# Low parts of the expert tables in the gate stage: from VectorE to GpSimd

## The reference

```python
act = jax.nn.gelu(jnp.einsum('td,tkd->tk', hx, u_tab[ix]))
return jnp.einsum('tk,tkd->td', gx * act, v_tab[ix])
```

## Time and profile before

| what | value |
|---|---|
| median of 3 runs | 3313.42 us (3311.34 to 3317.97) |
| the profiled execution, own time | 3313.91 us |
| its span | 3312.1 us, mean granted TensorE clock 0.951 |
| busy: TensorE / VectorE / ScalarE / GpSimd | 2998.8 / 2008.9 / 1268.6 / 138.2 us |
| gate stage, layer 0 and layer 1 | 531 to 677 us, 2221 to 2366 us |

### The profile page before, as it was taken

One profiled execution on the slowest core, in us unless ns is written; L12 is line 12 of the kernel. 1 busy time (PEld: TensorE's weight loads), 2 busy tenths in 40 slices (PEclk: granted clock), 3 DMA queues, 4 the chain that ended last, 5 costly groups with the idle time before them and its releaser, 6 DMA issues. The chain is left out here.

```text
span 3312.1 us, 48668 instructions
## 1 busy us (share of the span) xinstructions
PE 2998.8 (91%) x17552; PEld 2692.5 (81%) x17552; DVE 2008.9 (61%) x3884; ACT 1268.6 (38%) x1854; POOL 138.2 (4%) x108
## 2 busy tenths in 40 slices
PE   7957897899999999999877767987899999999997
PEld 4946797799999999988666666987899999999885
DVE  8867589944446666655569843789744444444454
ACT  3342445743333333333421124447633333333333
POOL 0000350000000000000000001510000000000000
PEclk9977899999999999999888877999999999999999
DMA  5703233664466666656300021325754444444463
GB/s 201 267 19 118 89 115 121 254 218 151 150 202 214 214 214 214 214 152 177 114 14 10 3 94 54 109 96 217 263 160 150 151 151 150 150 150 151 138 178 110
DMA packets 308862, 489.98 MB, mean 148 GB/s; under 512 B 214256, under 2 KB 215024, under 8 KB 304256
## 3 DMA queue, kind: packets, MB, share of 16 engines
q1 hardware_dynamic: 305856, 438.02, 40.8%
q10 hardware_dynamic: 2880, 50.33, 3.8%
HBM read 430.91 MB, written 57.38 MB: 147 GB/s over the span
## 5 line engine op out<-in xcount | busy, mean ns | idle before, releaser
L163 DVE TENSOR_TENSOR val_vl<-val_vr,val_vh 128x1024 fp32r<-128x1024 f32 x256 | 313.8, 1226 | 882.7 <-ACT val_vh L1828 882.7
L1665 PE MATMUL pe_s<-peer_hi,pe_uh 128*128 128x384 f32 x2304 | 784.8, 341 | 26.8 <-DVE peer_lo L163 15.9
L1667 PE MATMUL pe_s<-peer_hi,pe_ul 128*128 128x384 f32 x2304 | 775.9, 337 | 0.0
L1666 PE MATMUL pe_s<-peer_lo,pe_uh 128*128 128x384 f32 x2304 | 775.8, 337 | 0.0
L1763 ACT ACTIVATE pe_A<-pe_s 128x384 f32 (+1 forms) x256 | 126.1, 493 | 1124.2 <-PE pe_s L1667 1124.2
L1730 PE MATMUL peer_acc<-val_vh,val_wl 128*128 128x512 f32 x1536 | 474.2, 390 | 0.0
L1665 PEld LDWEIGHTS pe_s<-peer_hi,pe_uh 128*128 128x128 f32 x2304 | 436.5, 189 | 45.7 <-issue 23.0
L1730 PE MATMUL peer_acc<-val_vh,val_wh 128*128 128x512 f32 x1536 | 473.2, 389 | 0.0
L1730 PE MATMUL peer_acc<-val_vl,val_wh 128*128 128x512 f32 x1536 | 472.7, 389 | 0.0
L1666 PEld LDWEIGHTS pe_s<-peer_lo,pe_uh 128*128 128x128 f32 x2304 | 436.9, 190 | 8.4
L1667 PEld LDWEIGHTS pe_s<-peer_hi,pe_ul 128*128 128x128 f32 x2304 | 436.4, 189 | 0.0
(11 more groups left out here) (436 smaller groups left out, 3528.1 us busy)
## 6 DMA issues: line engine op xcount, KB each, us to landing
pe_ur<-in_peer_u SPq DMA_DIRECT2D x256, 512.0 KB, 3.6
val_vr<-in_peer_v SPq DMA_DIRECT2D x256, 512.0 KB, 4.4
val_gr<-gates SPq DMA_DIRECT2D x256, 192.0 KB, 4.6
val_mrow<-in_ada_rows SPq DMA_DIRECT2D x56, 512.0 KB, 4.1
gates<-gate_stg ACTq DMA_DIRECT2D x6, 4096.0 KB, 13.5
pe_ur<-in_w_query SPq DMA_DIRECT2D x32, 512.0 KB, 3.5
gates<-gate_stg ACTq DMA_DIRECT2D x4, 3072.0 KB, 12.8
in_w<-in_w_in SPq DMA_DIRECT2D x23, 512.0 KB, 4.6
```

Source lines behind the costliest of these rows:

```text
L163: return nc.vector.tensor_tensor(r32(out), x, hi, ALU.subtract)
L1665: pe.matmul(o, r32(uh[:, b, k]), r32(hi[:, k]), start=k == 0, stop=False)
L1666: pe.matmul(o, r32(uh[:, b, k]), r32(lo[:, k]), start=False, stop=False)
L1667: mm = pe.matmul(o, r32(ul[:, b, k]), r32(hi[:, k]), start=False, stop=k == KC - 1)
```

## The change

GpSimd gets the low parts of tables 18 to 33, one 128x1024 instruction each, behind a wait for the low part before and one for the table's high part. VectorE makes only one-hots in the groups, and waits for table 33's low part before it makes that of table 34.

```diff
@@ block.gpsimd
                         nc.gpsimd.tensor_tensor(r32(ul[:, b, h]), ur[:, b, h], uh[:, b, h], ALU.subtract).then_inc(ulow, 1)
+            for n in range(GATED, LAST):
+                pool.wait_ge(ulow2, n - LOW)
+                pool.wait_ge(uhigh2, n - LOW + 1)
+                nc.gpsimd.tensor_tensor(r32(ul[:, n % 2]), ur[:, n % 2], uh[:, n % 2], ALU.subtract).then_inc(ulow2, 1)
@@ block.vector
             table_low(GATED - 1, 1 - GATED % 2)
             for c in range(CHUNKS):
                 one_hots(c)
-                if c % GROUP == 1:
-                    n = GATED + c // GROUP
-                    table_low(n, n % 2)
...
             dve.sem_inc(vlow, 2)
             start = Slot(0, 0)
+            dve.wait_ge(ulow2, LAST - LOW)
             table_low(LAST, LAST % 2)
             dve.wait_ge(evacd, CHUNKS)
```

## The result

The changed kernel takes 3456.83 us (median of 4 runs, 3455.69 to 3457.31), the kernel before 3312.38 (4 runs): ratio 1.043, 95% interval 1.042 to 1.045. The forecast was 3451 us. The profiled execution has a span of 3454.8 us, 142.7 more than before. From the first one-hot to the clearing of PSUM layer 0's gate stage took 144.8 us (531.17 to 676.01) and takes 218.4 (528.03 to 746.39), 73.5 more: half of the whole loss. The other half is layer 1's stage, 71.0 more.

A forecast was written before the change was run, and what follows sets the result against it. Bound: a VectorE-TensorE loop of 8.79 us per gate group, without the low part. 3313.9 us plus 77.4 for GpSimd blocking VectorE and 60 for TensorE's lowered clock gave 3451 us; own range 3420 to 3480, wider range 3342 to 3480.

The forecast's parts named there:

- the block: Third chunk's one-hots in each gate group: GpSimd's low part stops VectorE 2.5 us, 3.7 in the first group; 77.4 us altogether.
- the clock: TensorE's gap before third-chunk matmuls grows from 1.7 to 4.2 us; clock halves in nearly every group, 2.0 us each, 60 us.
- Freeing VectorE is worth nothing: Gate groups: the 1.22 us low part is outside the 8.79 us VectorE-TensorE loop, so removing it from VectorE gains nothing.
- Who goes first: Third chunk's one-hots: GpSimd, having waited, goes in between VectorE's first and second or second and third instruction, adding 2.5 us.
- The rival with this mechanism: Gate groups: VectorE keeps its place through successive one-hots, GpSimd starts after them; loop 9.8 us, kernel 3350 us, chance 0.24.
- The rival without the clock: Gate groups: GpSimd goes in between one-hots, but the clock stays at 1.00; 3391 us, chance 0.12.
- The rival without a collision: Gate groups: one-hots leave GpSimd room, so its 2.5 us runs beside them; 3314 us, chance 0.09.

The follow-up runs named there:

- split kernel: Changed kernel with TensorE's order altered, half of each table's product moved ahead of the group's third-chunk matmuls, the other half behind: 3334.11 us, ratio 1.006.
- copy: Changed kernel with GpSimd copying the table into the low part (one read) instead of subtracting: 3355.86 us, ratio 1.013.
- GpSimd in the idle time: Changed kernel with GpSimd also waiting until the one-hots of the group's second chunk are done: 3349.52 us, ratio 1.011.
- low part in the middle: Kernel before, with VectorE making the low part amid the third chunk's one-hots instead of ahead of them: 3380.28 us, ratio 1.021.

## Why the prediction was right

The steps held in kind; two sizes were off and nearly offset each other: the block was put 10 us too high, the clock 17 us too low. That the sum came within 6 us of the time is in part luck.

- *Freeing VectorE is worth nothing.* Shown: without GpSimd's instruction 3312.0 us, VectorE idle for 1.5 us a group (1.57 predicted).
- *The block.* Said: 2.5 us in c2's one-hots, on the second or third instruction. It is 2.16 us on the third. GpSimd's 128x1024 instruction takes 2.37 us where nothing is in its way, not the 2.5 taken from two halves. The estimate from the ratio in the Trainium skill (GPSIMD Engine Reference, Elementwise — side-by-side cycle accounting), 2.4 us, was nearer. In the first group two blocks fall on c1, and c2 starts 9.2 us after the first one-hot instead of 6.0: 3.2 us, 3.7 predicted. The term came to 67 us instead of 77.4.
- *Who goes first.* I took it that the one that waits goes next, by one event. It held for all 32 tables of the changed kernel, yet it is no rule: the split kernel shows VectorE keeping its place for 7 us. The rival with this mechanism (3350 us, 0.24) was wrong for this kernel, but its mechanism exists, and no row that I had read told the two cases apart. In two of the other versions table 18 was kept out for some 2 us while VectorE made c1's one-hots. That this step came out right is luck in that sense.
- *The clock.* Said: it falls in nearly every group, at 2.0 us each, 60 us. It fell in 15 groups of each layer, the first one (gaps of 3.7 and 1.3 us in layer 0) included, and in layer 0 it cost 2.7 us each, since work ran at half speed for 5.8 us, a little over the 5.6 that I held for the upper end. All falls together cost 77 us. This is the term that was most mis-sized. My reason for the lower value, that the clock may fall only once work has begun, held for one fall of 30: in layer 1's second group it came 0.8 us after the work began and cost 1.6 us. In the others it came before, mostly by about a microsecond.
- *The rival without the clock* (3391 us) was reproduced by keeping TensorE busy: 3386 us.
- *The rival without a collision* fell with the stretched one-hot; only an instruction that does not read behaves so.

## What to carry to other kernels

Before moving work to an idle engine, find the loop or chain that sets the pace and ask whether the work is in it; here it was not, and an engine that was busy for 94% had slack where the work stood. Then ask at which moment the other engine will run it and what it shares with the engine that it relieves: the same GpSimd instruction cost 144 us in the loop and 36 us in VectorE's idle time, and a write in its place cost nothing. And price a longer gap on TensorE with the clock that follows it, not with its length alone.

## What the runs showed of the hardware

- The clock and the length of TensorE's gap, in groups of layer 0's gate stage: 1.7 us, no fall in 16 (the kernel before); 2.1 us, 3 of 5 (split kernel with GpSimd); 2.5 us, 6 of 15 (copy); 2.6 us, 6 of 8 (GpSimd in the idle time); 2.8 us, 8 of 15 (low part in the middle); 3.9 us, 14 of 14 (changed kernel). A fall cost 1.3 to 2.8 us. I had expected a clearer edge between falling and not falling.
- TensorE can be given useless work at a profit: 14 extra products per group made the changed kernel 71 us faster, and 7 made the kernel with the low part in the middle 32 us faster.
- GpSimd's reading instruction and VectorE's two-input instruction exclude each other, with one input (VectorE stood for 0.84 us) as with two (2.16 us); a write alone does not. Which of the two goes first when both have work is not fixed: GpSimd got in within 0.6 us in the changed kernel, and after up to 7 us in the split kernel.
